# Pairwise activation halves and dense products that run from the last column to the first

## The reference

```
x = first_block(x, ...)     # rms norm, projection to 5408 columns, RWKV-7 time mix,
                            # rotary attention, two sigmoid-gated branches, conv FFN of 2816
return second_block(x, ...) # forgetting attention + SwiGLU (2816), S5 state space mixer + SwiGLU (2816)
```

## Time and profile before

| | |
|---|---|
| median of 3 runs | 1154.11 us (1153.53 to 1157.0) |
| the profiled execution's own time | 1152.62 us |
| its span | 1150.8 us |
| PE, PEld, DVE, ACT, POOL busy | 96%, 79%, 68%, 52%, 10% |
| granted TensorE clock, mean over the span | 0.996 |
| read from HBM | 175.25 MB, 153 GB/s over the span |

### The profile page before, as it was taken

The page is one execution under the profiler, slowest core; times in us unless marked ns, Lnnn a source line. Parts: engine busy times, 40 slices in busy tenths (PEclk is TensorE's granted clock), DMA queues, the critical chain, the costliest instruction groups (busy, mean ns, idle before and its releaser), DMA issues.

```text
span 1150.8 us, 18422 instructions
## 1 busy us (share of the span) xinstructions
PE 1102.9 (96%) x7620; PEld 910.4 (79%) x7620; DVE 783.4 (68%) x1268; ACT 598.0 (52%) x927; POOL 119.6 (10%) x122
## 2 busy tenths in 40 slices
PE   7999999999999999999998999999999799999997
PEld 6777878777888888887877887878878688888786
DVE  6747874767677775658566896887578867555553
ACT  6566533243665663565655654445672267345441
POOL 0405050500000000000000000012105400000000
PEclk9999999999999999999999999999999999999999
DMA  8533322024654555555323654555531245555551
GB/s 316 183 115 121 129 75 75 21 74 146 200 184 165 183 178 189 183 166 192 122 90 110 255 185 151 182 198 190 175 130 58 76 165 183 189 180 190 192 200 57
DMA packets 49668, 177.50 MB, mean 154 GB/s; under 512 B 5648, under 2 KB 6288, under 8 KB 49328
## 3 DMA queue, kind: packets, MB, share of 16 engines
q1 hardware_dynamic: 49440, 175.79, 45.0%
q10 hardware_dynamic: 144, 0.52, 0.1%
HBM read 175.25 MB, written 1.05 MB: 153 GB/s over the span
## 4 chain that ended last, share of the span: by engine, by line
PE 79%; DVE 12%; ACT 6%; issue 2%; POOL 1%; DMA 0%; SPq 0%; DVEq 0%; ACTq 0%
PE wps L2679 22%; PE wps L2681 21%; PE wps L2680 21%; PE tps L2668 4%; DVE wlo L1817 3%; ACT whi L1420 1%; PE wps L3123 1%; PE tps L2909 1%; DVE arena L2039 1%; PE tps L2914 1%; PE tps L2725 1%; DVE bt L2434 1%; PE tps L3089 1%; DVE bt L2445 1%; PE tps L2886 1%
## 5 line engine op out<-in xcount | busy, mean ns | idle before, releaser
L1817 DVE TENSOR_TENSOR wlo<-raw,whi 128x1024 fp32r<-128x1024 f32 (+1 forms) x322 | 390.4, 1232 | 174.1 <-ACT whi L1420 172.7
L2679 PE MATMUL wps<-whi,a_hi 128*128 128x512 f32 (+1 forms) x1008 | 400.5, 397 | 4.6 <-DVE a_lo L1825 2.3
L2681 PE MATMUL wps<-wlo,a_hi 128*128 128x512 f32 (+1 forms) x1008 | 391.9, 389 | 0.0
L2680 PE MATMUL wps<-whi,a_lo 128*128 128x512 f32 (+1 forms) x1008 | 391.1, 388 | 0.0
L1420 ACT ACTIVATE whi<-raw 128x1024 fp32r<-128x1024 f32 (+1 forms) x322 | 327.2, 1053 | 76.2 <-PE wps L2681 76.1
L2679 PEld LDWEIGHTS wps<-whi,a_hi 128*128 128x128 f32 x1008 | 189.3, 188 | 45.7 <-issue 5.9
L2681 PEld LDWEIGHTS wps<-wlo,a_hi 128*128 128x128 f32 x1008 | 189.2, 188 | 40.1
L2680 PEld LDWEIGHTS wps<-whi,a_lo 128*128 128x128 f32 x1008 | 189.6, 188 | 36.8 <-issue 0.5
L2679 PE MATMUL wps<-whi,f_hi 128*128 128x512 f32 x264 | 103.3, 391 | 0.0
L2681 PE MATMUL wps<-wlo,f_hi 128*128 128x512 f32 x264 | 102.8, 389 | 0.0
L2680 PE MATMUL wps<-whi,f_lo 128*128 128x512 f32 x264 | 102.7, 389 | 0.0
(11 more groups left out here) (419 smaller groups left out, 1247.4 us busy)
## 6 DMA issues: line engine op xcount, KB each, us to landing
raw<-in_w_dn SPq DMA_DIRECT2D x22, 512.0 KB, 3.2
raw<-in_w_0dn SPq DMA_DIRECT2D x22, 512.0 KB, 3.2
raw<-in_w_1dn SPq DMA_DIRECT2D x22, 512.0 KB, 3.2
raw<-in_w_ua SPq DMA_DIRECT2D x20, 512.0 KB, 3.2
raw<-in_w_ub SPq DMA_DIRECT2D x20, 512.0 KB, 3.3
raw<-in_w_0ug SPq DMA_DIRECT2D x20, 512.0 KB, 3.3
raw<-in_w_0uu SPq DMA_DIRECT2D x20, 512.0 KB, 3.3
raw<-in_w_1ug SPq DMA_DIRECT2D x20, 512.0 KB, 3.2
```

The costliest lines, as they stand in the source:

```text
L1817: V.tensor_tensor(t.wlo[n % NR][:, 0:w], t.raw[n % NR][:, 0:w], t.whi[n % NH][:, 0:w].bitcast(F32), ALU.subtract).then_inc(m.done(s.dve_lo ...
L2679: T.matmul(o, xh, wh, start=first, stop=False)
L2680: T.matmul(o, xl, wh, start=False, stop=False)
L2681: mm = T.matmul(o, xh, wl, start=False, stop=last)
```

## The change

Three things. The two halves of an activation share one buffer of twice the length, word by word: element s of the high half is word 2s of its tile, element s of the low half word 2s + 1. So every read and write of a half steps by two words (8 bytes). Second, `product` takes the columns of the streamed weights and of the PSUM sums in descending order (step -1) for all three matmuls, which leaves each sum at its place. Third, `over`'s tables are laid out anew, since tiles 0 to 11 of `f1` now are words 0 to 6143 of the shared bytes: both halves of `t.cp` lie there, `t.cp3` and the first `t.near` behind them. Which instructions there are on each engine, their order, their sizes and the semaphores they wait for are the same in both kernels; buffers keep their total size.

```diff
@@ place
-    a_hi, a_lo = sb("a_hi", [P, 8, S], F32R), sb("a_lo", [P, 8, S], F32R)
+    pair = sb("a_pair", [P, 8, S, 2], F32R)
+    a_hi, a_lo = (pair[:, :, :, i] for i in range(2))
...
     def hidden(name, stack):
-        t.acts[name] = (sb(name + "_hi", [P, 22, S], F32R, stack), sb(name + "_lo", [P, 22, S], F32R, stack))
+        pair = sb(name + "_pair", [P, 22, S, 2], F32R, stack)
+        t.acts[name] = tuple(pair[:, :, :, i] for i in range(2))
...
-        t.cp = [over[:, c0:c0 + 3072].rearrange("p (i r k c) -> p i r k c", i=16, r=2, k=3) for c0 in (0, 5632)]
-        t.cp3 = over[:, 3072:5120].rearrange("p (i r c) -> p i r c", i=32, r=2)
-        t.near = [over[:, c0:c0 + 384].rearrange("p (k d c) -> p k d c", k=4, d=3) for c0 in (5120, 10752)]
+        t.cp = [over[:, c0:c0 + 3072].rearrange("p (i r k c) -> p i r k c", i=16, r=2, k=3) for c0 in (0, 3072)]
+        t.cp3 = over[:, 6144:8192].rearrange("p (i r c) -> p i r c", i=32, r=2)
+        t.near = [over[:, c0:c0 + 384].rearrange("p (k d c) -> p k d c", k=4, d=3) for c0 in (8192, 10752)]
@@ product
-        T.matmul(o, xh, wh, start=first, stop=False)
-        T.matmul(o, xl, wh, start=False, stop=False)
-        mm = T.matmul(o, xh, wl, start=False, stop=last)
+        T.matmul(o[:, ::-1], xh, wh[:, ::-1], start=first, stop=False)
+        T.matmul(o[:, ::-1], xl, wh[:, ::-1], start=False, stop=False)
+        mm = T.matmul(o[:, ::-1], xh, wl[:, ::-1], start=False, stop=last)
```

## The result

The changed kernel takes 1179.7 us (1178.54 to 1180.97, four runs) where the one before takes 1155.55 (1153.53 to 1162.31, four runs): 24.2 us more between the medians. The ratio over all the runs is 1.0194 with a 95% interval of 1.0147 to 1.0242, or 22.4 us: **slower**, by about 2%. The forecast was 1154 and the range ended at 1174. The profiled execution took 1180.97 us (before 1152.62) over a span of 1179.2 (1150.8), at a mean granted clock of 0.992 (0.996).

A forecast was written before the change was run, and what follows sets the result against it. The prediction took the number of matmuls times the distance between their starts on PE as the bound. All terms were 0: 1152.6 us plus 0, plus 1.5 us for the median, gave 1154 us, range 1147 to 1174.

The forecast's parts named there:

- The weight load reads every second word: Weight loads of the products: even at half speed hidden behind 512 columns; 0, ends 0 and +4 us.
- The stream and the sums go downwards: Streamed weights and PSUM sums of `product`: descending words stay neighbours, so no change.
- the 14 ns between two products: Time between products beyond their columns: unknown, might shrink or grow, ends from 0 to twice 14 ns.
- Half pace downwards: Rival, every product: a descending column takes two cycles, 213 ns more each, 690 to 813 us slower; chance 0.17.
- at half pace 24 x 107 ns = 2.6 us: The 24 matmuls of `forget_mm` streaming stepped halves: 2.6 us at half pace, otherwise nothing; taken as 0.
- ACT and DVE write every second word: Writes of the halves by ACT and DVE: stepped writes cost nothing, 0, with +11 us kept as an end.
- The doubling that I kept as an end: Stepped writes of ACT and DVE costing double per element, of which 11 us would reach the end.
- One ns more or less per product is worth 3.2 to 3.8 us: Distance between product starts: each ns changes the kernel's time by 3.2 to 3.8 us, 0.3%.
- A small toll: Rival: double-cost writes (+11 us), starts 2 to 5 ns longer (+6 to +19), or short products and `forget_mm` paying; 0.14.
- The new places in `over`: The tables of `over`: only addresses alter, `t.cp` and `t.cp3` wait for the same as before; 0.
- no wait is new: All engines and queues: no instruction added, removed or moved, so no shifted transfer and no new queueing.
- what is left over in both is 14 ns a matmul: Distances at 512 and 288 columns: one 2.4 GHz cycle a column plus 14 ns a matmul.

The follow-up runs named there:

- e1_pairs: The kernel before with the halves side by side word by word and `over` as changed, products ascending; ratio 1.0162.
- e4_sums: The kernel before with only the PSUM sums written downwards, weight columns laid out in reverse before launch, halves apart; ratio 1.0020.
- e3_stream: The kernel before with only the streamed weights read downwards, weight columns laid out in reverse before launch, halves apart; ratio 1.0125.
- e9_narrow_up: The kernel before with products of six feed-forward groups computing only their first 480 to 320 columns, halves apart, ascending; 1117.86 us, one run.
- e18_before_64B: The kernel before with `a_hi` and `a_lo` moved up by 64 bytes, nothing else changed; distance of products loading from them 227.7 to 233.3 ns.

## Why the prediction was wrong, step by step

- **"The weight load reads every second word ... I take 0, ends 0 and +4 us"** failed, and its upper end too. The argument was that a load has 227 ns of cover and would stay hidden even at half speed. The load itself behaved: its row went from 188 to 197 ns, and the 288-column products stayed at 132. But hidden is not free: with loads that read every second word, 512-column products stand 6 to 8 ns further apart (e1_pairs, 1.0162).
- **"The stream and the sums go downwards ... I take no change"** held for the sums (e4_sums, 1.0020, with 1 in the interval) and failed for the stream (e3_stream, 1.0125). The unknown that I named, the 14 ns between two products, is where it shows, and my bound of "from 0 to twice 14 ns" held it: 14 became 20. But these ends never reached the range: 14 ns more would be 45 to 53 us by the prediction's own price, and the rival and the range took 2 to 5 ns, for which no row spoke.
- **Half pace downwards** (0.17): refuted, 233 ns and not 440. Half pace does exist, and stood beside the case where I gave it the 2.6 us: **`forget_mm`** "at half pace 24 x 107 ns = 2.6 us, otherwise nothing. I take 0". It took 231 ns where it had 120, the upper end to the tenth. By the Trainium skill ("Advanced Engine Details and Errata", "Memory Cachelines": two hits on a line of 16 bytes are enough) an 8-byte step streams at full pace; the trace says half, for what streams through the array.
- **ACT and DVE write every second word**: "I take 0" held for DVE (686 to 689 ns for 512 elements). ACT pays about 0.1 ns an element, 381 to 395 ns for 128, 596 to 655 for 512: its busy time grew by 3.4 us, of which nothing can be found in PE's waits. The doubling that I kept as an end belongs, for ACT, to a step of 16 bytes (596 to 1127); DVE's 686 became 1105 there.
- **"One ns more or less per product is worth 3.2 to 3.8 us"** held: the traces show 22.8 us for 6.3 ns, 3.6 us per ns; with `forget_mm`'s 2.6 us it makes 25, and 24.2 was measured between the medians. This is the sum that should have been made for the small toll.
- **A small toll** (0.14) was thus the right case with a term too small: "a product's start costs 2 to 5 ns more (+6 to +19 us)". It was 6.3 ns, +20 to +24 us. The range ended at 1174 because of it.
- **"The new places in `over` ... 0", "no wait is new"**: right; PE's wait for a low half is 2.4 us for 2.3.

The deeper fault lies ahead of these: "what is left over in both is 14 ns a matmul" was read from three widths of one layout as if it were a property of the chip. It was a property of that layout (e9_narrow_up, e18_before_64B), and none of the layouts tried went below its 227 ns at 512 columns. With 0.3% of the time on each ns, and no row for any other step, direction or place, that asked for more than 0.31 on slower.

## What to carry to other kernels

In a kernel bound by a row of matmuls, price each edit in ns of distance between two starts first, and treat every change of address, step or direction of what is loaded or streamed as one that can cost 6 ns of 227; hold those buffers contiguous and at the places where the distance was measured, and measure the distance again after anything moves them, even a filler of 64 bytes. The direction in which PSUM is written is free (e4_sums). Don't stream an operand with a step of 8 bytes (half pace), nor load or write with one of 16; where two halves must lie side by side, the writers hardly mind a step of 8 (ACT 10% more, DVE under 1%).

## What the runs showed that I had not expected

- A shift of one buffer by 64 bytes costs 5.6 ns on each product that loads from it (227.7 to 233.3), and nothing on others.
- Two tolls of 6 ns, from a stepped load and from a descending stream, together make 6 to 7 ns (233.3 to 233.9).
- The pairs' toll comes and goes with the width: none at 504 columns, 6 ns at 510. At 508 columns, stretches of one trace go at 226.8 or at 233.3 ns, also where all their buffers are the same. The ascending, contiguous distance lies up to 5 ns above its own line at 448 columns (204.9 in the mean against 200.1) and on it at 512.
- Steps of 8 bytes: a stream goes from 120 to 231 ns for 256 columns, a load from 188 to 194 or 197, ACT's write from 596 to 655, DVE's from 686 to 689. Steps of 16 bytes: 233, 312, 1127 and 1105 ns.
